# Group norms of a chunked recurrence moved to other places of the program, and the last norm's block merged into the chunks' block

## The reference, cut to what matters

```python
    _, ys = lax.scan(step, S0, xs)                    # the recurrence, 512 steps, 8 heads of 64
    y = jnp.moveaxis(ys, 0, 1)
    mean = jnp.mean(y, axis=-1, keepdims=True)
    var = jnp.mean(jnp.square(y - mean), axis=-1, keepdims=True)
    y = ((y - mean) * lax.rsqrt(var + RW_GN_EPS)).reshape(B, T, RW_WIDTH) * ln_w + ln_b
    bonus = jnp.sum(rh * kh * r_k, axis=-1, keepdims=True) * vh
    y = y + bonus.reshape(B, T, RW_WIDTH)
    return (y * g).astype(zr.dtype)                   # g = sigmoid(gl) @ g2
...
    merged = gates[:, :, 0] * (y_r @ p_rwkv[l]) + gates[:, :, 1] * (y_n @ p_nsa[l])
    h = h + gt1 * (merged @ w_out[l])
```

## Time and profile before

| | us |
|---|---|
| median of 3 runs | 1183.73 |
| lowest and highest run | 1181.54, 1189.93 |
| the profiled execution's own time | 1183.8 |
| its span in the trace | 1181.9 |
| TensorE busy | 1034.2 |
| VectorE busy | 419.3 |
| ScalarE busy | 205.9 |
| GpSimd busy | 149.5 |

### The profile page before, as it was taken

One profiled execution on the slowest core, in us unless ns is written; L12 is line 12 of the kernel. 1 busy time (PEld: TensorE's weight loads), 2 busy tenths in 40 slices (PEclk: granted clock), 3 DMA queues, 4 the chain that ended last, 5 costly groups with the idle time before them and its releaser, 6 DMA issues.

```text
span 1181.9 us, 13401 instructions
## 1 busy us (share of the span) xinstructions
PE 1034.2 (88%) x5421; PEld 504.1 (43%) x5421; DVE 419.3 (35%) x736; ACT 205.9 (17%) x441; POOL 149.5 (13%) x219
## 2 busy tenths in 40 slices
PE   5999999999998898998999759998888787788786
PEld 4443344445445565766455424433333333333232
DVE  4663446563082653457424541111110110110016
ACT  4011123333102564232111100000000000000003
POOL 4100001141200444212000010010000000000000
PEclk8999999999999999999999869998899999989998
DMA  9923427324936200100973569999999999999995
GB/s 350 384 96 107 163 87 278 110 72 172 248 102 152 42 1 30 36 2 2 367 282 139 217 216 429 429 425 426 427 427 427 427 427 428 426 425 428 426 381 200
DMA packets 73936, 301.81 MB, mean 255 GB/s; under 512 B 21446, under 2 KB 27944, under 8 KB 61329
## 3 DMA queue, kind: packets, MB, share of 16 engines
q1 hardware_dynamic: 60354, 280.11, 59.9%
q0 software_dynamic: 6912, 15.59, 3.4%
q10 hardware_dynamic: 6608, 5.24, 1.5%
HBM read 286.03 MB, written 22.03 MB: 261 GB/s over the span
## 4 chain that ended last, share of the span: by engine, by line
PE 30%; DMA 12%; issue 3%; SPq 3%; DVE 3%; ACT 1%; DVEq 0%; ACTq 0%; POOLq 0%
PE ps L2638 13%; PE ps L2661 7%; PE ps L2579 5%; DMA uT<-in_moe_w_down_dram 4%; DMA ring<-in_moe_w_down_dram 4%; DMA zrT<-in_moe_w_down_dram 4%; PE ps L2530 3%; SPq L2059 3%; DMA uT<-y_dram 1%; PE ps L2621 1%; PE ps L2546 1%; PE ps L2648 0%; DVE h L2438 0%; ACT hdT L2196 0%; DMA zrT<-u_dram,slots 0%
## 5 line engine op out<-in xcount | busy, mean ns | idle before, releaser
L2638 PE MATMUL ps<-ring,zrT 128*64 128x512 f32 x624 | 203.3, 644 | 47.6 <-issue 46.2
L1047 PE MATMUL ps<-ring,uT 128*128 128x512 f32 x384 | 170.9, 599 | 0.6 <-PE ps L965 0.6
L2638 PEld LDWEIGHTS ps<-ring,zrT 128*64 128x64 f32 x624 | 67.0, 148 | 176.7 <-issue 176.7
L1036 PE MATMUL ps<-uT,ring 128*128 128x512 f32 x256 | 116.3, 611 | 2.0 <-DVE uT L701 1.4
L2394 DVE TENSOR_TENSOR cst<-cst,ps 128x512 f32<-128x512 f32 x16 | 11.0, 687 | 296.2 <-PE ps L2638 296.2
L1047 PEld LDWEIGHTS ps<-ring,uT 128*128 128x128 f32 x384 | 71.9, 191 | 87.2 <-issue 86.6
L2661 PE MATMUL ps<-ring,hdT 128*64 128x512 f32 x320 | 92.1, 594 | 12.0 <-ACT hdT L2196 7.9
L1036 PEld LDWEIGHTS ps<-uT,ring 128*128 128x128 f32 x256 | 48.9, 195 | 66.2 <-issue 64.9
L2404 DVE TENSOR_TENSOR zrT<-ps,mod 128x512 f32<-128x512 f32 x32 | 22.1, 692 | 110.3 <-PE ps L2661 110.1
L2661 PEld LDWEIGHTS ps<-ring,hdT 128*64 128x64 f32 x320 | 31.0, 137 | 61.1 <-issue 61.1
L2638 PE MATMUL ps<-mg,zrT 128*64 128x512 f32 x96 | 45.7, 632 | 11.7 <-issue 11.7
(11 more groups left out here) (434 smaller groups left out, 1382.7 us busy)
## 6 DMA issues: line engine op xcount, KB each, us to landing
ring<-in_moe_w_gate_dram SPq DMA_DIRECT2D x20, 2048.0 KB, 37.1
ring<-in_moe_w_up_dram SPq DMA_DIRECT2D x18, 2048.0 KB, 38.2
ring<-in_moe_w_down_dram SPq DMA_DIRECT2D x18, 2048.0 KB, 38.1
ring<-in_w_in_dram SPq DMA_DIRECT2D x8, 2048.0 KB, 12.6
ring<-in_w_ada_dram SPq DMA_DIRECT2D x8, 2048.0 KB, 9.0
ring<-in_w_ada_dram SPq DMA_DIRECT2D x16, 512.0 KB, 13.3
zrT<-in_moe_w_up_dram SPq DMA_DIRECT2D x3, 2048.0 KB, 42.1
mod<-in_moe_w_gate_dram SPq DMA_DIRECT2D x3, 2048.0 KB, 41.4
```

Of the source, the lines that this page charges most:

```text
L1036: ins = pe.matmul(ps[:, n % 4, :], slot(name, KD, w)[:, k, c0:c0 + P], uT[:, k, :], start=(k == 0), stop=(k == KD - 1))
L1047: ins = pe.matmul(ps[:, n % 4, :], uT[:, k, P * i:P * i + P], w, start=(k == 0), stop=(k == KD - 1))
L2638: ins = pe.matmul(ps[HALF * r:HALF * r + HALF, "gu".index(kind), :], xgT[:, k, HALF * r:HALF * r + HALF], w[r][:, k, :], start=(k == 0), s ...
```

## The change

It reorders the norms and moves the last one, with the gating and the turning of the rows, into the chunks' block.

- Chunk 0's norm runs whole on VectorE behind the masked tiles `b_out(3, 1)`, ahead of `low_rows(1, 0)`. ScalarE's square and root for it stand behind the copy of chunk 1's `y`, and GpSimd's bonus stands between its `diagonals` of the first and second pair.
- Chunk 1's steps 0 and 1 stand behind `low_rows(1, 0)` and `low_rows(1, 1)`; its steps 2 to 4 behind `w_out(2)`. Between the second pair's `k_out` calls stands no norm step any more. ScalarE squares between its two halves of the second `low_product` copies.
- Chunk 2's norm follows `w_out(3)`; its square and root stand ahead of the copy of chunk 3's `y`.
- Chunk 3's norm, `g` and `gated` follow in the same block. One meeting of the engines goes.
- The transposes of three chunks stand ahead of the last `nsa_product`, those of the fourth behind it, with ScalarE's copies, all ahead of the merge's block. The merge's block starts with the `p_rwkv` products.

```diff
@@ -1332,7 +1332,11 @@
-        q_ld, q_yc, q_sq, q_v, q_s, q_yb, q_done = (sem(f"q_{n}") for n in "ld yc sq v s yb done".split())
+        q_ld, q_yc, q_sq, q_v, q_s, q_yb, q_done, q_g, q_fin = (
+            sem(f"q_{n}") for n in "ld yc sq v s yb done g fin".split())
+
+        m_yT, m_yTe = sem("m_yT"), sem("m_yTe")
+        yrT = zrT[:, 0:4, :]
...
@@ -1469,10 +1473,13 @@
                 for c in range(NT):
+                    if c == 2:
+                        pool.wait_ge(g_diag, 12)
+                        norm_bonus(pool, link, 0)
+                        pool.wait_ge(q_yb, 1)
                     diagonals(c)
                 pool.wait_ge(g_diag, 6 * NT)
-                norm_bonus(pool, link, 0)
-                for i in range(1, NT - 1):
+                for i in range(1, NT):
                     norm_bonus(pool, link, i)
...
                 for k in range(2):
-                    for q_ in range(2):
-                        low_rows(k, q_)
+                    low_rows(k, 0)
                     if k:
-                        normed(0, 0)
+                        normed(1, 0)
+                    low_rows(k, 1)
+                    if k:
+                        normed(1, 1)
                     for q_ in range(2):
                         low_block(k, q_)
                     k_out(2 * k, 0)
-                    if k:
-                        normed(0, 1)
                     for q_ in range(2):
                         dve.wait_ge(g_t2, 2 * k + q_ + 1)
                         r = halves[1]
                         dve.tensor_copy(t1[q_][r, :, :, :], wide8(2 + q_)[r, :, :, :]).then_inc(g_t2e, 1)
                     k_out(2 * k, 1)
-                    if k:
-                        normed(0, 2)
                     k_out(2 * k + 1, 0)
                     k_out(2 * k + 1, 1)
                     w_out(2 * k)
                     if k:
-                        normed(0, 3)
-                        normed(0, 4)
-                        normed(1, 0)
-                    state_out(2 * k)
-                    if k:
-                        normed(1, 1)
-                    w_out(2 * k + 1)
-                    if k:
                         normed(1, 2)
                         normed(1, 3)
                         normed(1, 4)
+                    state_out(2 * k)
+                    w_out(2 * k + 1)
                     if k == 0:
                         dve.wait_ge(g_y, 1)
                         b_out(2, 0)
...
@@ -1571,8 +1570,25 @@
                         dve.wait_ge(g_y, 2)
                         b_out(3, 0)
                         b_out(3, 1)
+                        for step in range(5):
+                            normed(0, step)
+
+                def gated(i):
+                    dve.wait_ge(q_done, i + 1)
+                    dve.wait_ge(q_g, i + 1)
+                    dve.tensor_tensor(yr(i), yr(i), by_tile(ps[:, i, :]), ALU.mult).then_inc(q_fin, 1)
+
                 for step in range(5):
                     normed(2, step)
+                normed(NT - 1, 0)
+                gated(0)
+                normed(NT - 1, 1)
+                gated(1)
+                normed(NT - 1, 2)
+                gated(2)
+                normed(NT - 1, 3)
+                normed(NT - 1, 4)
+                gated(NT - 1)
...
@@ -1584,15 +1600,16 @@
                             .then_inc(g_t1A, 1)
+                        if k and q_ == 0:
+                            norm_square(act, 1)
+                    if k:
+                        norm_root(act, 1)
                     act.wait_ge(g_x0, 4)
...
                                 .then_inc(g_x1A, 1)
-                    if k:
-                        norm_square(act, 0)
-                        norm_root(act, 0)
                     for q_ in range(2):
...
@@ -1603,17 +1620,23 @@
                         act.activation(usb, ps[:, 2, :].rearrange("p (h d) -> p h d", h=HEADS), ACT.Copy).then_inc(g_ue, 1)
-                        if c == 2:
-                            norm_square(act, 1)
+                        if c == NT - 1:
+                            norm_square(act, 2)
+                            norm_root(act, 2)
                         act.wait_ge(g_y, c + 1)
                         for p_ in range(2):
                             act.activation(y[:, c, :, HD * p_:HD * p_ + HD],
...
                                 .then_inc(g_ye, 1)
-                        if c == 2:
-                            norm_root(act, 1)
-                norm_square(act, NT - 2)
-                norm_root(act, NT - 2)
+                        if c == 1:
+                            norm_square(act, 0)
+                            norm_root(act, 0)
+                norm_square(act, NT - 1)
+                norm_root(act, NT - 1)
+                for n in range(NT):
+                    act.wait_ge(m_yT, n + 1)
+                    act.activation(yrT[:, :, P * n:P * n + P], ps[:, n, :].rearrange("p (j t) -> p j t", j=4), ACT.Copy)\
+                        .then_inc(m_yTe, 1)
...
@@ -1790,47 +1813,17 @@
                 recur(2)
                 recur(3)
                 nsa_product(pe, 0, 6)
-                pe.wait_ge(g_ye, 2 * NT)
-        chunk.close()
-
-
-        q_g, q_fin, q_dve, q_pool = (sem(f"q_{n}") for n in "g fin dve pool".split())
-
-        with nc.Block() as block:
-            @block.gpsimd
-            def _(pool):
-                norm_bonus(pool, Chain(pool, q_pool), NT - 1)
-
-            @block.scalar
-            def _(act):
-                norm_square(act, NT - 1)
-                norm_root(act, NT - 1)
-
...
-                norm_step(dve, link, NT - 1, 0)
-                gated(0)
-                norm_step(dve, link, NT - 1, 1)
-                gated(1)
-                norm_step(dve, link, NT - 1, 2)
-                gated(2)
-                norm_step(dve, link, NT - 1, 3)
-                norm_step(dve, link, NT - 1, 4)
-                gated(NT - 1)
-
-            @block.tensor
-            def _(pe):
                 pe.wait_ge(q_ld, 48)
                 for i in range(NT):
                     pe.matmul(ps[:, i, :], zrT[:, 13, P * i:P * i + P], g2[:, :], start=True, stop=True).then_inc(q_g, 1)
-                nsa_product(pe, 1, 7)
+                for n in range(NT):
+                    if n == NT - 1:
+                        nsa_product(pe, 1, 7)
+                    pe.wait_ge(q_fin, n + 1)
+                    for j in range(4):
+                        ins = pe.transpose(ps[:, n, P * j:P * j + P], yr(n)[:, j, :], ident)
+                    ins.then_inc(m_yT, 1)
+        chunk.close()
...
@@ -2094,7 +2086,6 @@
                 pool.memset(eps[:, :], 1e-6).then_inc(f_eps, 1)
-                pool.wait_ge(m_yTe, NT)
                 pool.dma_start(grow2, A["norm_ffn_g"][0].partition_broadcast(P)).then_inc(m_g, 16)
...
@@ -2151,10 +2142,6 @@
-                for n in range(NT):
-                    act.wait_ge(m_yT, n + 1)
-                    act.activation(yrT[:, :, P * n:P * n + P], ps[:, n, :].rearrange("p (j t) -> p j t", j=4), ACT.Copy)\
-                        .then_inc(m_yTe, 1)
                 for n in range(8):
...
@@ -2500,12 +2487,6 @@
                 ident = C("ident")
-                for n in range(NT):
-                    src = yr(n)
-                    for j in range(4):
-                        ins = pe.transpose(ps[:, n, P * j:P * j + P], src[:, j, :], ident)
-                    ins.then_inc(m_yT, 1)
-                pe.wait_ge(m_yTe, NT)
```

More of the change, by code:

```diff
@@ L1792, in _ @@
                 nsa_product(pe, 0, 6)
-                pe.wait_ge(g_ye, 2 * NT)
-        chunk.close()
-        q_g, q_fin, q_dve, q_pool = (sem(f"q_{n}") for n in "g fin dve pool".split())
-        with nc.Block() as block:
-            @block.gpsimd
-            def _(pool):
-                norm_bonus(pool, Chain(pool, q_pool), NT - 1)
-            @block.scalar
-            def _(act):
-                norm_square(act, NT - 1)
-                norm_root(act, NT - 1)
-            @block.vector
-            def _(dve):
-                link = Chain(dve, q_dve)
-                def gated(i):
-                    dve.wait_ge(q_done, i + 1)
-                    dve.wait_ge(q_g, i + 1)
-                    dve.tensor_tensor(yr(i), yr(i), by_tile(ps[:, i, :]), ALU.mult).then_inc(q_fin, 1)
-                norm_step(dve, link, NT - 1, 0)
-                gated(0)
-                norm_step(dve, link, NT - 1, 1)
-                gated(1)
-                norm_step(dve, link, NT - 1, 2)
-                gated(2)
-                norm_step(dve, link, NT - 1, 3)
-                norm_step(dve, link, NT - 1, 4)
-                gated(NT - 1)
-            @block.tensor
-            def _(pe):
                 pe.wait_ge(q_ld, 48)
@@ L1863, in build @@
         gcol2 = alloc(top, "gcol2", [P, KD])
-        yrT = zrT[:, 0:4, :]
         mgT = uT[:, :, :]
@@ L1868, in build @@
         u2 = mg[:, 0:2, :]
```

(4 more changed lines are left out.)

## The result

| | before | changed |
|---|---|---|
| median, both measured on one chip | 1184.04 us | 1190.43 us |
| lowest and highest of 20 runs each | 1179.94, 1189.93 | 1181.09, 1194.06 |
| the profiled execution's span | 1181.9 | 1192.1 |
| mean granted clock of TensorE in it | 0.952 | 0.938 |

The prediction was 1183.3 us with a range up to 1187.5: wrong. The runs aren't spread evenly: one took 1181.09, ten lie between 1188.48 and 1190.45, nine between 1193.30 and 1194.06. The mean granted clock of the nine was 0.938 to 0.946, that of the ten 0.947 to 0.952, and that of the 1181.09 was 0.953.

A forecast was written before the change was run, and what follows sets the result against it. Expert-weight streaming sets the end, so shifts of the first merge product on TensorE's path arrive undiminished. +1.5 - 0.4 - 1.65 + 0.1 = -0.45 us on 1183.8 gave 1183.3, range 1180.5 to 1187.5.

The forecast's parts named there:

- Part 1: Chunk 0's norm on VectorE under the attention products: done at 520.65, before anyone needs it, cost 0.
- Part 2: Chunk 1's first steps delay ScalarE's copy of `t`; TensorE's second `low_blocks` loses 1.5 us, between 0.3 and 2.0.
- Part 3: No norm step between the `k_out` calls: TensorE's last wait falls from 1.78 to 1.38, 0.4 us gained.
- Part 4: Tail, last chunk's product to first merge product: 14.9 us instead of 16.6, 1.6 to 1.7 gained, bounds 0.9 and 2.1.
- Part 5: Gate-row reads at the merge block's start: first lands at 4.9 us; TensorE's third tile loses 0.1, between 0 and 2.0.
- The noise: Whole kernel's time: no difference below about 1%, or 12 us, shows; its three runs lie 8 us apart.
- the clock falls: Rival, chance 0.06: new waits in `low_blocks` or between transposes lower TensorE's clock, costing 0.7 us, so 1184.05.
- the old wait of 1.78 us: Second pair, TensorE waiting for VectorE behind the last `k_gram`'s masked tiles; matmuls behind it kept their usual length.

The follow-up runs named there:

- norms_alone: Kernel before with only the norms of chunks 0 to 2 moved, chunk 1's first steps behind both copies of `t`, tail blocks kept separate; 1181.29 us.
- bonus_held: Changed kernel with GpSimd's bonus for chunk 1 held until VectorE has ended that chunk's subtraction; 1183.22 us, ratio 1.0025.
- wait_of_one_us: Kernel before with three chained ScalarE copies added ahead of the second pair's second copy of `t`; 1184.74 us, ratio 0.9998.
- wait_of_1_5_us: Kernel before with four chained ScalarE copies added ahead of the second pair's second copy of `t`; 1192.27 us, ratio 1.0065.
- before_with_wait: Kernel before with five chained ScalarE copies added ahead of the second pair's second copy of `t`, no norm moved; 1194.35 us, ratio 1.0098.
- tail_alone: Kernel before with only the merged block (last norm, gates, turned rows), the norms of chunks 0 to 2 left in place; 1184.59 us, ratio 1.0013.

## Why the prediction was wrong, step by step

- **Part 1** held: chunk 0's nine steps ran from 515.24 to 521.44, 6.20 us where 6.25 were forecast, and nobody waited for them. The table load took its 1.28 us, to 518.81, and the root began at 518.83: no other time went with it.
- **Part 2** had the right chain and place and 1.5 us for a stop of 2.17, outside its own upper bound of 2.0, the only part to leave its bounds. I had written 1.85 for VectorE's step 0 with GpSimd beside it; it took 2.63, from 521.92 to 524.55, for the subtraction. By itself this is +0.7.
- **Part 3** held: the last wait is 1.38, as forecast.
- **Part 4** held: 14.64 us for 14.9, even to the wait of 0.36 between the transposes (0.4 forecast). But the 1.49 that I took for the price of a block end was mostly the wait for chunk 2's norm, as norms_alone shows (0.30), so the gain was laid to the merging where most of it is the early norm's.
- **Part 5** held: VectorE's first multiplication starts 4.62 us behind the merge's first product, released by the DMA (4.9 forecast), and TensorE doesn't stop.
- **The noise**: I had written that this kernel shows no difference below about 1%. With 20 runs of each, 0.6% is clear of it.

The step that failed: the sum lets the new stop cost its own length and gives the low clock behind it nothing. The clock stands only in the rival "the clock falls", with a chance of 0.06 and a price of +0.7 us. I priced a fall by the 32 matmuls of a block's start, where the clock is back 3.0 us behind the first of them, and wrote -0.45 + 0.7. The fall at `low_blocks` lasted 23.9 us and cost 9.9 in the profiled execution. With that price the rival reads 1193, and it is slower, not the same. The 0.7 us of part 2 alone would have left the sum at +0.2, inside the range.

The argument against it was that behind the old wait of 1.78 us the matmuls ran at their usual length. That was one row of one execution, at another place. The runs show that it covers nothing: at that very kind of wait the clock fell in bonus_held (1.37 us, at 495.1) and in wait_of_one_us (1.45 us, at 536.4). And at `low_blocks` more runs are long with a longer stop, without a sharp edge:

| stop at `low_blocks` in the profiled execution, us | kernel | clock in that execution | runs above 1190, of all |
|---|---|---|---|
| 0.71 | wait_of_one_us | held at this stop | 0 of 10 |
| 1.16 | bonus_held | fell 2.0 us behind TensorE's new start | 3 of 12 |
| 1.37 | wait_of_1_5_us | fell 0.3 us behind it | 8 of 10 |
| 2.04 | before_with_wait | fell 0.4 us ahead of it | 6 of 6 |

Of the kernel before, 3 of 103 runs lay above 1190 (0 of 20, 1 of 29, 2 of 35, 0 of 19). The mark isn't quite the same for all rows, since bonus_held has the tail's gain, and its three need not all come from this stop, as the clock fell at two places in the one with a trace.

The changed kernel, with 2.17, has 11 of 20 above 1190 and eight more between 1188.48 and 1189.56. What it gained elsewhere (1.94 in the tail, 0.4 at the last wait) is in these. The upper group lies within 0.8 us, 4 above the lower; what parts the two was not isolated, since only one execution, of the upper group, has a trace.

I had named the wait in `low_blocks` as a place where the clock could fall, but not as the likeliest. "TensorE: Matmul & The Clock Gate" of the Trainium skill, section "Part 4: PE-mode transpose", says that transposes don't count as work for the gate; by it I called the tail the likeliest place. In the changed kernel the tail kept its clock (1.00 in 566:576, with twelve transposes and a wait of 0.36 us). In `tail_alone`, where three waits stood between the transposes, it fell there, which agrees with the rule but doesn't single it out from the waits.

Why the clock stays low so long behind `low_blocks` (20.5 us in bonus_held, 23.9 in the other three traces with a fall here) stays open. At a block's start it is back 3 to 6 us behind the first matmul, and the falls at the `vt,gk` waits and in the tail of tail_alone lasted about 3.5 us. In all four traces with a fall at `low_blocks` (after, before_with_wait, wait_of_1_5_us and bonus_held) it comes back at the same place of the program, `recur(2)`'s second `state` products, whichever time that is: 549.9, 547.7, 544.4 and 549.7. What decides that wasn't tried.

## What to carry to other kernels

Where a change puts a new wait on TensorE, even of little over 1 us, price it with two numbers: its length, and the stretch behind it at half clock. That stretch cost 1.4 us at one place of this kernel and 9.9 at another. A row of before where a longer wait did no harm is no cover; in other places and other executions the clock fell. The cheap cure here was to let the wait not arise (one line in another engine's list, 1181.09 us), or to fill it with matmuls without use (1181.62), and to keep work off the engine whose copy TensorE waits for until that copy is done.

## What the runs showed of the hardware

- A TensorE stop of 1.37 us amid small matmuls (32x32, 64x256) brought 8 of 10 runs above 1190 us; in the one that has a trace the clock was at 1.2 GHz instead of 2.4 for 23.9 us. The fall isn't tied to the moment of the new start: it came 0.3 and 0.4 us ahead of it (after stops of 2.17 and 2.04), and 0.3, 1.8 and 2.0 us behind it (1.37, 1.45 and 1.16).
- GpSimd's `TENSOR_TENSOR` of 128x512 holds back a VectorE `TENSOR_TENSOR` with two SBUF inputs: 1.70 us for 0.69, and 0.69 again when bonus_held moved GpSimd's away. It also held a `TENSOR_SCALAR` of 128x8 for 1.13 us, which takes 0.17, and which ended 0.03 us behind GpSimd's; no run tested this one by itself. A `TENSOR_REDUCE` beside it kept its 0.69. "GPSIMD Engine Reference" of the Trainium skill, section "1. Specifications", says that the two engines contend where VectorE has two SBUF inputs or uses a 2-port mode; the first of the three agrees, and no row here shows which mode the second was in.
- A block's first 32 matmuls took 5.15 to 5.41 us in five traces and 6.68 to 6.76 in six, of the same instructions behind the same 2.13 us of idle time; with one matmul more ahead of the block end, and 1.48 us of idle time, they took 3.73.
